# Norm sums moved to GpSimd at four stage starts, three weight pieces along, scratch operands in PSUM, fewer identity products

## The reference

```
h = rms_norm_2(x, n_pre_mix)
proj = h @ w_in
...
x = x + rms_norm_2(merged @ w_o, n_post_mix)
h = rms_norm_2(x, n_pre_ffn)
gu = h @ w_ffn_gu
ffn = (silu(gu[..., :D_FF]) * gu[..., D_FF:]) @ w_ffn_down
return x + rms_norm_2(ffn, n_post_ffn)
```

## Time and profile before

| | |
|---|---|
| median of 3 runs | 3596.87 us (3594.16 to 3602.26) |
| the profiled execution's own time | 3596.7 us |
| its span | 3594.9 us |
| TensorE busy | 97% |
| VectorE, ScalarE, GpSimd busy | 65%, 40%, 10% |
| DMA, mean | 166 GB/s |

### The profile page before, as it was taken

One profiled execution on the slowest core, in us unless ns is written; L12 is line 12 of the kernel. 1 busy time (PEld: TensorE's weight loads), 2 busy tenths in 40 slices (PEclk: granted clock), 3 DMA queues, 4 the chain that ended last, 5 costly groups with the idle time before them and its releaser, 6 DMA issues. The chain is left out here.

```text
span 3594.9 us, 47480 instructions
## 1 busy us (share of the span) xinstructions
PE 3500.2 (97%) x18217; PEld 2993.1 (83%) x18224; DVE 2325.5 (65%) x4211; ACT 1430.5 (40%) x2390; POOL 352.1 (10%) x280
## 2 busy tenths in 40 slices
PE   8999999999999899999999999999999999999998
PEld 6776778999999899999977767788877776778887
DVE  6656766889899789888734556554334555654433
ACT  4343343433899533333323234333222323443221
POOL 1000000000233434333100000000000000000000
PEclk9999999999999999999999999999999999999999
DMA  4321243555899999999622224233332223423332
GB/s 150 103 65 48 68 138 104 199 169 170 288 365 367 377 359 402 381 385 381 250 88 77 81 86 144 88 100 100 94 88 89 85 72 86 155 77 106 100 93 72
DMA packets 213172, 597.38 MB, mean 166 GB/s; under 512 B 22258, under 2 KB 80404, under 8 KB 211412
## 3 DMA queue, kind: packets, MB, share of 16 engines
q1 hardware_dynamic: 176084, 460.13, 38.5%
q0 software_dynamic: 36864, 134.23, 9.7%
HBM read 523.36 MB, written 69.21 MB: 165 GB/s over the span
## 5 line engine op out<-in xcount | busy, mean ns | idle before, releaser
L580 ACT ACTIVATE stream_hi<-stream_raw 128x1024 fp32r<-128x1024 f32 (+1 forms) x611 | 638.8, 1046 | 1072.8 <-PE ffn_ps L2826 416.9
L588 DVE TENSOR_TENSOR stream_lo<-stream_raw,stream_hi 128x1024 fp32r<-128x1024 f32 (+1 forms) x611 | 739.9, 1211 | 440.8 <-ACT stream_hi L580 432.8
L1158 PE MATMUL experts_ps<-mix_a_hi,stream_hi 128*128 128x384 f32 x1024 | 342.8, 335 | 16.0 <-issue 16.0
L616 PE MATMUL experts_ps<-h_hi,stream_hi 128*128 128x384 f32 x1024 | 346.7, 339 | 1.1 <-PEq L746 1.1
L1158 PE MATMUL experts_ps<-mix_a_lo,stream_hi 128*128 128x384 f32 x1024 | 342.6, 335 | 0.0
L1158 PE MATMUL experts_ps<-mix_a_hi,stream_lo 128*128 128x384 f32 x1024 | 342.5, 334 | 0.0
L616 PE MATMUL experts_ps<-h_lo,stream_hi 128*128 128x384 f32 x1024 | 342.2, 334 | 0.0
L616 PE MATMUL experts_ps<-h_hi,stream_lo 128*128 128x384 f32 x1024 | 342.2, 334 | 0.0
L2824 PE MATMUL mid_ps<-h_hi,stream_hi 128*128 128x512 f32 x672 | 281.5, 419 | 4.0 <-PEq L3054 2.2
L2824 PE MATMUL ffn_ps<-h_hi,stream_hi 128*128 128x512 f32 x704 | 280.7, 399 | 2.7 <-DVE h_lo L2880 2.7
L2826 PE MATMUL ffn_ps<-h_hi,stream_lo 128*128 128x512 f32 x704 | 274.0, 389 | 0.0
(11 more groups left out here) (510 smaller groups left out, 6832.8 us busy)
## 6 DMA issues: line engine op xcount, KB each, us to landing
stream_raw<-u SPq DMA_DIRECT2D x128, 512.0 KB
stream_raw<-v SPq DMA_DIRECT2D x128, 512.0 KB
stream_raw<-l_gu SPq DMA_DIRECT2D x88, 512.0 KB
expert_hidden<-experts_gelu SPq DMA_DIRECT2D x128, 192.0 KB
expert_weights<-built SPq DMA_DIRECT2D x12, 2048.0 KB
built<-expert_weights SPq DMA_DIRECT2D x16, 1536.0 KB
stream_raw<-l_gate SPq DMA_DIRECT2D x48, 512.0 KB
built<-expert_hidden SPq DMA_DIRECT2D x124, 192.0 KB
```

The source lines that it names most:

```text
L580: self.nc.scalar.activation(self.hi[n % self.RING][:, 0:w], self.raw[n % self.RAW][:, 0:w], ACT.Copy).then_inc(self.hi_done, 1)
L588: self.nc.vector.tensor_tensor(self.lo[n % self.RING][:, 0:w], self.raw[n % self.RAW][:, 0:w], self.hi[n % self.RING][:, 0:w].bitcast(F32) ...
L616: mm = self.nc.tensor.matmul(self.ps[n % 2], a, b[:, k, :], start=(k == 0 and m == 0), stop=(k == DC - 1 and m == 2))
L1158: mm = nc.tensor.matmul(out[d][:, DIRECT:SEQ], v, a[b % RING][:, :], start=(b == 0 and m == 0), stop=(b == KEYS - 1 and m == 2))
```

## The change

It has these parts.

- Project and ffn: the product of ones with each row's squares goes. GpSimd adds the squares of all eight rows into row 0 of m (`gather` with all rows), and one product of ones follows the pieces (`total_of_one`).
- The first three pieces are worked on along with the rows (`in_order` with an order written out) instead of the first two. The low part of the third piece is made by GpSimd (`low_by_pool`), ahead of its adds. High and low of pieces 3 and 4 are made before root and reciprocal.
- `scale` writes to two banks of PSUM in turn (`scaled_at`) instead of m, and `add` reads them. ScalarE makes x times gain once more, unrounded, in two other banks (`fresh`), and the low part is that minus the high part (`low_of_fresh`), a plain subtraction.
- `update` begins with scale 0, add 0, scale 1, add 1, low 0.
- `Leaving`: both groups of small products accumulate in the same columns; `join` goes, `root` reads PSUM.
- Identity products: 2 instead of 8 at the ends of the attention stages, 6 instead of 12 at the start of merge.

```diff
@@ paired_attention
-                idle_products(nc, C, turned[0], 8)
+                idle_products(nc, C, turned[0], 2)
@@ class Stream
+    def low_by_pool(self, pool, n):
+        w = self.width(n)
+        pool.wait_ge(self.hi_done, n + 1)
+        self.nc.gpsimd.tensor_tensor(self.lo[n % self.RING][:, 0:w], self.raw[n % self.RAW][:, 0:w],
                                      self.hi[n % self.RING][:, 0:w].bitcast(F32), ALU.subtract).then_inc(self.lo_done, 1)
@@ class Residual
     def scale(self, dve, k):
...
-        self.nc.vector.tensor_tensor(self.m[:, k, :], self.m[:, k, :], self.by_token.ps, ALU.mult).then_inc(self.scaled, 1)
+        if k >= 2:
+            dve.wait_ge(self.added, k - 1)
+        self.nc.vector.tensor_tensor(self.scaled_at[k % 2], self.m[:, k, :], self.by_token.ps, ALU.mult).then_inc(self.scaled, 1)
 
     def add(self, dve, k):
         dve.wait_ge(self.scaled, k + 1)
-        self.nc.vector.tensor_tensor(self.x[:, k, :], self.x[:, k, :], self.m[:, k, :], ALU.add).then_inc(self.added, 1)
+        self.nc.vector.tensor_tensor(self.x[:, k, :], self.x[:, k, :], self.scaled_at[k % 2], ALU.add).then_inc(self.added, 1)
...
+    def low_of_fresh(self, dve, k):
+        dve.wait_ge(self.hi_done, k + 1)
+        dve.wait_ge(self.fresh_done, k + 1)
+        self.nc.vector.tensor_tensor(self.lo[:, k, :], self.fresh_at[k % 2], self.hi[:, k, :].bitcast(F32),
+                                     ALU.subtract).then_inc(self.lo_done, 1)
+
+    def fresh(self, act, k):
+        if k >= 2:
+            act.wait_ge(self.lo_done, k - 1)
+        self.nc.scalar.activation(self.fresh_at[k % 2], self.x[:, k, :], ACT.Copy,
+                                  scale=self.gain[:, k:k + 1]).then_inc(self.fresh_done, 1)
...
+    def total_of_one(self, pe, ps):
+
+        pe.wait_ge(self.gathered, DC - 1)
+        self.nc.tensor.matmul(ps, self.C.ones[:, :], self.m[:, 0, :], start=True, stop=True).then_inc(self.summed, DC)
...
+ENDING = [(j, k) for j in range(3) for k in (6, 7)]
+ROW_BY_ROW = [(j, k) for k in range(6) for j in range(3)] + ENDING
+THIRD_LATER = ([(j, k) for k in range(2) for j in range(2)] + [(2, 0), (2, 1)]
+               + [(j, k) for k in range(2, 6) for j in range(3)] + ENDING)
@@ class Leaving, total
-            self.nc.tensor.matmul(ps[:, t:t + 1], self.acc[:, tokens], self.C.ones[:, 0:1], start=True, stop=True)
+            self.nc.tensor.matmul(ps[:, t:t + 1], self.acc[:, tokens], self.C.ones[:, 0:1], start=(t == 0), stop=False)
...
-    def join(self, dve, ps):
-        dve.wait_ge(self.summed, 1)
-        self.nc.vector.tensor_reduce(self.tok, ps[:, 0:2 * TT].rearrange("p (a t) -> p t a", a=2), AX_X, ALU.add).then_inc(self.joined, 1)
@@ project
-                idle_products(nc, C, bank[3], 12 if res.adds else 9)
-                res.first_two(pe, stream, first, bank, total)
-                for n in range(2, N_PROJECT):
+                idle_products(nc, C, bank[0], 12 if res.adds else 9)
+                res.in_order(pe, stream, first, bank, ROW_BY_ROW if res.adds else THIRD_LATER)
+                res.total_of_one(pe, total)
+                for n in range(3, N_PROJECT):
...
+            @block.gpsimd
+            def _(pool):
+                stream.low_by_pool(pool, first + 2)
+                res.gather(pool, DC)
...
+def begin(act, res, stream, first):
+    if res.adds:
+        stream.high(act, first + 2)
+    for k in range(DC):
+        res.high(act, k)
+        res.fresh(act, k)
+        if k == 0 and not res.adds:
+            stream.high(act, first + 2)
+        res.square(act, k)
+    stream.high(act, first + 3)
+    stream.high(act, first + 4)
...
 def update(dve, res, stream, first):
     if res.adds:
         res.scale(dve, 0)
-    for k in range(DC):
+        res.add(dve, 0)
+        res.scale(dve, 1)
+        res.add(dve, 1)
+        res.low_of_fresh(dve, 0)
+        res.scale(dve, 2)
+    for k in range(2, DC):
         if res.adds:
             if k + 1 < DC:
                 res.scale(dve, k + 1)
             res.add(dve, k)
-        if k >= 1:
-            res.low(dve, k - 1)
-        if k == 5:
-            stream.low(dve, first + 2)
-    res.low(dve, DC - 1)
+        elif k == 2:
+            res.low_of_fresh(dve, 0)
+        res.low_of_fresh(dve, k - 1)
+    res.low_of_fresh(dve, DC - 1)
+    stream.low(dve, first + 3)
+    stream.low(dve, first + 4)
@@ merge_and_out
-                idle_products(nc, C, bank[6], 12)
+                idle_products(nc, C, bank[6], 6)
```

More of the change, by code:

```diff
@@ L3125, in _ @@
                 res.invert(dve)
-                stream.low(dve, first + 3)
-                take(0)
-                take(1)
-                for n in range(2, N_PROJECT):
+                for n in range(3):
+                    take(n)
+                for n in range(3, N_PROJECT):
                     stream.low(dve, first + n + 2)
@@ L3245, in _ @@
                             leave.ready_root(act)
-                leave.root(act)
+                leave.root(act, total)
             @block.vector
@@ L3295, in _ @@
                         leave.add(dve, d)
-                leave.join(dve, total)
                 leave.invert(dve)
@@ L3332, in _ @@
                 res.by_token.rows(pe, bank[7])
-                idle_products(nc, C, bank[5], 12)
-                res.first_two(pe, stream, first, bank, x_total)
-                for n in range(2, N_GU):
+                idle_products(nc, C, bank[0], 12)
+                res.in_order(pe, stream, first, bank, ROW_BY_ROW)
+                res.total_of_one(pe, x_total)
+                for n in range(3, N_GU):
                     if n >= BANKS:
@@ L3369, in high @@
                     nc.scalar.activation(a_hi[:, i, :], both_of(i), ACT.Copy).then_inc(a_hi_done, 1)
-                for k in range(DC):
-                    res.high(act, k)
-                    res.square(act, k)
-                    if k == 4:
-                        stream.high(act, first + 2)
+                begin(act, res, stream, first)
                 res.root(act, x_total)
-                stream.high(act, first + 3)
                 silu(0)
                 for n in range(2, N_GU):
-                    stream.high(act, first + n + 2)
+                    if n >= 3:
+                        stream.high(act, first + n + 2)
                     if n % 2 == 0:
@@ L3394, in _ @@
                             leave.ready_root(act)
-                leave.root(act)
+                leave.root(act, m_total)
             @block.vector
@@ L3421, in _ @@
                 for n in range(2, N_GU):
-                    stream.low(dve, first + n + 2)
+                    if n >= 3:
+                        stream.low(dve, first + n + 2)
                     take(n)
@@ L3434, in _ @@
                             leave.add(dve, d)
-                leave.join(dve, m_total)
                 leave.invert(dve)
```

54 lines of the change are left out of this document (24 added, 30 removed).

## The result

The changed kernel took 3568.28 us (median of 4 runs, 3565.22 to 3569.75) beside 3599.57 for the kernel before on the same chip (with a fourth run of it, 3604.74): ratio 0.9914, 95% interval 0.9902 to 0.9925.

A forecast was written before the change was run, and what follows sets the result against it. TensorE, busy 97% of the span, was taken to bound the kernel. Terms of 24.3 + 0 + 5.2 + 2.2 + 0 = 31.7 us gave 3565.0 from the profiled 3596.7, or 3565.2 as median; range 3559 to 3577.

The forecast's parts named there:

- Products of ones: Starts of project and ffn: seven pairs of ones leave TensorE, 6.1 us per stage; 24.3 us taken over four.
- VectorE's and ScalarE's rows: Loops at the starts: VectorE 1.80 and ScalarE 1.83 us a row, within TensorE's 2.05, so no cost.
- First row: Three starts with adds: TensorE begins 0.2 us sooner, then waits 0.3; together 0, bounds -0.3 to +0.8 per stage.
- GpSimd: At the starts: adds of 1.29 to 1.55 us, third piece's low part 2.6 to 3.1; nothing waits.
- End of the norm: Ones pair through first take needs 5.85 us; TensorE has 6.3 of work in project, 0.3 to 0.4 spare.
- Hand-overs: Attention ends gain 5.2 us, merge starts 2.2; dropping the join at merge and ffn ends gains 0, at most 0.8.
- Clock: Granted clock after idles, as at the start of "up": 0 charged, with -2 to +4 us.
- contention: VectorE operations beside GpSimd take 1.58 us despite PSUM: 3607, chance 0.04; milder, one of three stretched: 3579, chance 0.09.
- fewer identity products let the clock fall: Six hand-overs with fewer identity products: if each costs 1.6 us, 9.6 come back, giving 3575; chance 0.10.
- The rival of the norm's chain: TensorE waits about 1 us in each project stage and 0.5 in the others: 3568; chance 0.10.

The follow-up runs named there:

- the two runs of the parts: Identity products cut alone on the kernel before: 3591.02 us, ratio 0.9978; changed kernel with 8 and 12 identity products put back: 3574.70 us, 0.9936.

## Why the prediction was right

The forecast was 3565.2 from a sum of 31.7 us; the profiled execution, which the sum is made against, gained 31.5, and the medians differ by 31.3. The median of 3568.28 lies 3.1 above the forecast mostly because that of the kernel before is 3599.57 with its fourth run, where the forecast stood on 3596.87. The mechanisms held, as the points show; that the two profiles agree with the sum to 0.2 us is luck, since stretches that were not changed differ between them by up to 3.4 us. Point by point:

- **Products of ones**: 7 pairs of 0.88, 6.1 a stage, were to go; 6.32 went in each stage with adds and a full clock, and 5.94 in the first project stage. The 6.32 are 7 x 0.88 = 6.2 for the pairs and 0.19 for the earlier first product, so all else together, the pitch of 0.23 for which I took 0.2 off and the wait at the second row, cost less than 0.1.
- **VectorE's and ScalarE's rows**: 1.80 forecast, 1.79 measured; scale and low 0.68 to 0.69 into and out of PSUM, no cost for the place. ScalarE 1.79 against 1.83. The page's 62 cycles for a PSUM source ("VectorE: DVE Perf Modes", section on the TRN2 errata, of the Trainium skill) don't show: VectorE's add takes 679 ns with a PSUM source, and 0.69 with both in SBUF and nobody beside it.
- **First row**: 0 in sum, from 0.2 gained and 0.3 waited. The first product came 0.19 sooner; the wait at the second row was about 0.15.
- **GpSimd**: adds of squares 1.29 as said; its low part took 2.36 where I estimated 2.6 to 3.1 from the slower of its adds. Neither is waited for.
- **End of the norm**: in the first project stage the pair of ones, the takes and the first product of piece 4 stand so:

```profile
1807.96 1.02 PE L2940 MATMUL mid_ps<-m_rows,stream_const 128*128 128x512 f32 x2
...
1813.34 1.89 DVE L3141 TENSOR_TENSOR y<-mid_ps,x_rstd 128x512 f32<-128x512 f32 x3
...
1814.27 0.39 PE L2830 MATMUL mid_ps<-h_hi,stream_hi 128*128 128x512 f32 x1
```

  The first of the three takes (0.69 us) ends at 1814.03, 0.24 ahead of piece 4, and TensorE doesn't wait. It fits, with less to spare than the 0.3 to 0.4 of the prediction: from the pair to the reciprocal it took 1.99 and not 1.78, as ScalarE's table load (1.28 us, to 1809.21), which had no row in my chain, ended just ahead of root (1809.23).
- **Hand-overs**: 1.29 for 1.30, 1.07 for 1.1, the join 0 for 0; the two runs with one product at these ends show that the reason given for the 0 was the right one.
- **Clock**: 0 charged, with -2 to +4. Half-clock stretches moved about: before 180 and 474 us, after 296 and 3180, and the stretch from 1960 to 2080 us was granted 0.91 where it had been 0.94. Up to the end of dil, ahead of the first changed instruction, the changed kernel's profile is 3.37 us shorter; in the nsa stage it is 2.86 longer. The terms as measured sum to 5.2 + 2.1 + 3 x 6.3 + 5.9 = 32.1, 31.5 arrived, so all this comes to 0.6 lost.
- **The rivals**: contention was excluded by the changed kernel's rows, and the run with the operands in SBUF shows how near it lay: the same loops without the PSUM operands give back some 15 of the 24 us. Its price in the prediction, 1.58 for every instruction, was too high: the delay is the rest of GpSimd's instruction, and not every one is met. That fewer identity products let the clock fall is not borne out at the places where the change cut them; where a run left out all 12 ahead of a longer idle, the clock was at half for longer. The rival of the norm's chain had 3568, which is also the median that was measured, but not its mechanism: TensorE waits nowhere before piece 4, and the 0.15 at the second row is its longest wait in these loops.

What the two runs of the parts leave: the change is worth 7.4 us by fewer products that nobody needs, and about 24 us by the sum on GpSimd, for which three along and PSUM operands are the conditions: without the one some 19 of the 24 are lost, without the other some 15.

## What to carry to other kernels

Work moved to GpSimd was free here only while VectorE's instructions beside it had no second input in SBUF; where PSUM banks are idle, put one operand there first. When an engine is busy 97% of the time, look for instructions in its queue that another engine can do within the row's pitch, and feed it enough independent work (a third piece) to cover that pitch. Identity products cost nothing where they hide under another engine's work ahead of a start, and there they may be worth their place through the clock; at a hand-over where TensorE ends last they were cost without a gain that these runs show. The difference of starts across the hand-over tells which case it is.

## What the runs showed of the hardware

- With two SBUF inputs, VectorE waits for GpSimd's instruction to end, and the other way round: an add of 0.69 took 2.17 us beside GpSimd's 2.35, ending 0.55 after it, and GpSimd's add of 1.29 took 1.71 when VectorE came first.
- VectorE and ScalarE write PSUM as fast as SBUF in these shapes: the scale takes 0.69 into PSUM and 0.68 into SBUF on VectorE (128x512, float32), and x times gain 0.67 into PSUM (float32) against 0.72 into SBUF (as the high part, fp32r) on ScalarE.
- GpSimd's subtraction of 128x1024 takes 2.35 us, its addition of 128x512 1.29.
- With an idle of 3.74 us behind the spreading products the granted clock over 10.2 us was 0.50, 0.83 and 0.51 at three starts; in the two at half clock it had fallen ahead of the idle, with the spreading products. In the changed kernel, with 12 identity products in that gap and 1.15 us of idle, the first ffn start was granted 1.00 and the second 0.83.
